# Eight weight chunks of the adaLN modulation move from VectorE to GpSimd and ScalarE inside the softmax heads

## The reference, cut to what matters

```
mod = silu(c) @ w_ada + b_ada            # 2048 x 12288, split into sh_a, sc_a, g_a, sh_m, sc_m, g_m
h = rms_norm(x) * (1 + sc_a) + sh_a ;  p = h @ w_in
A: latent attention, 8 heads (softmax)   B: stick-breaking, 8 heads   C: forgetting attention, 8 heads (softmax)
x = x + g_a * (concat(head norms of A, B, C) @ w_out)
h = rms_norm(x) * (1 + sc_m) + sh_m ;  x = x + g_m * (relu(h @ w1)^2 @ w2) ;  final rms_norm
```

## Time and profile before

| what | value |
|---|---|
| median of 3 runs | 1148.61 us (1147.33 to 1149.9) |
| the profiled execution's own time | 1150.71 us |
| its span in the trace | 1148.9 us |
| TensorE busy | 1101.0 us, 96% |
| VectorE busy | 724.6 us, 63% |
| ScalarE busy | 530.3 us, 46% |
| GpSimd busy | 309.3 us, 27% |

### The profile page before, as it was taken

One profiled execution on the slowest core, in us unless ns is written; L12 is line 12 of the kernel. 1 busy time (PEld: TensorE's weight loads), 2 busy tenths in 40 slices (PEclk: granted clock), 3 DMA queues, 4 the chain that ended last, 5 costly groups with the idle time before them and its releaser, 6 DMA issues.

```text
span 1148.9 us, 21562 instructions
## 1 busy us (share of the span) xinstructions
PE 1101.0 (96%) x9084; PEld 1072.9 (93%) x9084; DVE 724.6 (63%) x866; ACT 530.3 (46%) x657; POOL 309.3 (27%) x158
## 2 busy tenths in 40 slices
PE   7989999888999989999999999999999999999995
PEld 6889998886889989999999999999999999999995
DVE  5688676869886559787786444545555555445443
ACT  4644443564555445444544334343444444344341
POOL 3879996775138950000000000000000000000000
PEclk9999999999999998999999999999999999999998
DMA  9999998699777983888886565565556656555631
GB/s 382 416 415 415 415 400 331 220 347 376 249 256 288 410 310 131 301 287 296 291 301 204 190 201 188 198 191 196 192 192 200 191 187 202 196 190 194 199 117 74
DMA packets 76703, 296.87 MB, mean 258 GB/s; under 512 B 8512, under 2 KB 8640, under 8 KB 72512
## 3 DMA queue, kind: packets, MB, share of 16 engines
q1 hardware_dynamic: 76608, 295.50, 71.2%
HBM read 293.37 MB, written 2.10 MB: 257 GB/s over the span
## 4 chain that ended last, share of the span: by engine, by line
PE 80%; DMA 7%; DVE 6%; issue 4%; ACT 2%; SPq 0%; POOL 0%; DVEq 0%; ACTq 0%; POOLq 0%
PE ps L1310 50%; PE ps L1316 25%; DMA ada<-in_ada 4%; DMA ada_more<-in_whole 3%; PE ps L1328 2%; DVE ada L892 2%; PE ps L1492 1%; DMA ada<-in_whole 1%; PE ps L1333 1%; DVE qk L958 1%; ACT w_hi L465 1%; DVE ada_more L892 0%; DVE tmp L929 0%; ACT o_tok L698 0%; PE ps L1359 0%
## 5 line engine op out<-in xcount | busy, mean ns | idle before, releaser
L465 ACT ACTIVATE w_hi<-raw 128x1024 fp32r<-128x1024 f32 x362 | 380.6, 1059 | 466.2 <-PE ps L1316 420.5
L870 DVE TENSOR_TENSOR w_lo<-raw,w_hi 128x1024 fp32r<-128x1024 f32 x256 | 312.7, 1229 | 274.8 <-ACT w_hi L465 274.1
L1310 PE MATMUL ps<-hT,w_hi 128*128 128x256 f32 x3072 | 384.8, 278 | 12.7 <-issue 8.4
L1310 PEld LDWEIGHTS ps<-hT,w_hi 128*128 128x128 f32 x3072 | 367.2, 189 | 16.0 <-issue 9.5
L764 POOL TENSOR_TENSOR w_lo<-raw,w_hi 128x1024 fp32r<-128x1024 f32 x106 | 256.3, 2440 | 54.3 <-ACT w_hi L465 53.7
L1310 PE MATMUL ps<-act,w_hi 128*128 128x256 f32 x2048 | 253.2, 276 | 0.0
L1310 PEld LDWEIGHTS ps<-act,w_hi 128*128 128x128 f32 x2048 | 241.8, 188 | 0.1
L1316 PE MATMUL ps<-hT,w_lo 128*128 128x256 f32 x1536 | 207.4, 278 | 0.0
L758 POOL TENSOR_TENSOR ssq<-ssq,sq 128x1024 f32<-128x1024 f32 x6 | 14.4, 2404 | 658.2 <-ACT sq L472 658.2
L1316 PEld LDWEIGHTS ps<-hT,w_lo 128*128 128x128 f32 x1536 | 190.6, 189 | 0.0
L1316 PE MATMUL ps<-act,w_lo 128*128 128x256 f32 x1024 | 136.9, 276 | 0.0
(11 more groups left out here) (217 smaller groups left out, 797.4 us busy)
## 6 DMA issues: line engine op xcount, KB each, us to landing
raw<-in_weights SPq DMA_DIRECT2D x362, 512.0 KB, 4.5
ada<-in_ada SPq DMA_DIRECT2D x128, 512.0 KB, 5.4
ada<-in_whole SPq DMA_DIRECT2D x16, 1024.0 KB, 11.9
ada_more<-in_whole SPq DMA_DIRECT2D x16, 1024.0 KB, 12.7
xT<-in_xt SPq DMA_DIRECT2D x4, 512.0 KB, 7.1
y<-tmp SPq DMA_DIRECT2D x2, 512.0 KB, 2.8
consts<-in_consts SPq DMA_DIRECT2D x1, 580.0 KB, 9.8
y<-sq SPq DMA_DIRECT2D x1, 512.0 KB, 3.0
```

Of the source, the lines that this page charges most:

```text
L465: sc.activation(w_hi[:, u % RING, :, :], raw[:, u % LOADS, :, :], ACT.Copy).then_inc(hi_done, 1)
L870: ve.tensor_tensor(w_lo[:, slot, :, :], raw[:, u % LOADS, :, :], w_hi[:, slot, :, :].bitcast(F32), ALU.subtract).then_inc(lo_vec, 1)
L1310: pe.matmul(acc[:, n, :], w, rhs[:, kt0 + k, half, :], start=first and k == 0 and n % 2 == 0 and half == 0, stop=False, skip_group_check=True)
```

## The change

Eight of the twenty chunks among the softmax heads, the odd ones from 83 to 97, are taken out of DVE's queue. POOL multiplies chunk by `c` in place (`chunk_product`), with the SBUF copy `c_rep`; ACT then copies the buffer onto itself with an accumulator output (`sum_product`) into a column of `pool_sum`. Afterwards one DVE instruction adds the eight sums and their `plus_one` terms into `part_sum`. The load that reuses the buffer of such a chunk (`load_ada` of 87, 89, ..., 101) waits for ACT's sum instead of DVE's chunk. All other waits on `ada_done` are counted anew by `ada_count`.

POOL does products 0 and 1 after `fox_operand(7)`, products 2 to 5 between the two scalings by the head norm, and products 6 and 7 after the second. ACT does sum 0 at the end of step H+7, right behind `copy_pt(5)`, and the others in steps H+8, 9, 11, 13, 14, 16 and 17.

```diff
+POOL_AT, POOL_N = 33, 8
+SUM_AT = (7, 8, 9, 11, 13, 14, 16, 17)
+def pool_index(a):
+    m = a - A_X - POOL_AT
+    return m // 2 if 0 <= m < 2 * POOL_N and m % 2 == 0 else None
+def ada_count(a):
+    return sum(1 for n in range(a) if pool_index(n) is None)
...
             def load_ada(a):
-                if a >= WHOLE:
-                    sp.wait_ge(ada_done, ada_before(a) + 1)
+                n = pool_index(ada_before(a))
+                if n is not None:
+                    sp.wait_ge(pool_summed, n + 1)
+                elif a >= WHOLE:
+                    sp.wait_ge(ada_done, ada_count(ada_before(a) + 1))
...
+            def sum_product(n):
+                room = ada_room(A_X + POOL_AT + 2 * n)
+                sc.wait_ge(pool_made, n + 1)
+                sc.activation(room, room, ACT.Copy, accum_out=pool_sum[:, n:n + 1]).then_inc(pool_summed, 1)
...
                     copy_pt(t - H - TURN_LAG)
+                for n in range(POOL_N):
+                    if t == H + SUM_AT[n]:
+                        sum_product(n)
...
+            def chunk_product(n):
+                a = A_X + POOL_AT + 2 * n
+                gp.wait_ge(ada_landed(a), 16 * ada_round(a))
+                if n >= 2:
+                    gp.wait_ge(pool_made, n - 1)
+                gp.tensor_tensor(ada_room(a), ada_room(a), c_rep[:, D // 2:D], ALU.mult).then_inc(pool_made, 1)
+            gp.wait_ge(c_kept, 1)
+            chunk_product(0)
+            chunk_product(1)
             for n, at in enumerate((AT_SB, AT_FX)):
+                if n == 1:
+                    for i in range(2, POOL_N - 2):
+                        chunk_product(i)
                 gp.wait_ge(head_scaled, n + 1)
...
+            for n in range(POOL_N - 2, POOL_N):
+                chunk_product(n)
             for j in range(U_OUT - LAG):
                 lo(B_OUT + LAG + j)
...
             for t in range(STEPS):
-                todo = list(ada_at(t))
+                todo = [a for a in ada_at(t) if pool_index(a) is None]
...
+            ve.wait_ge(pool_summed, POOL_N)
+            ve.tensor_tensor(part_sum[:, POOL_AT:POOL_AT + 2 * POOL_N:2], pool_sum[:, :],
+                             plus_one[:, KT + 1:2 * KT:2], ALU.add).then_inc(pool_merged, 1)
+            ve.wait_ge(pool_merged, 1)
             out_lo(2)
...
-                    pe.wait_ge(ada_done, A_OUT)
+                    pe.wait_ge(ada_done, ada_count(A_OUT))
```

More of the change, by code:

```diff
@@ L189, in hybrid_block @@
         part_sum = sb("part_sum", [P, 6 * KT])
+        pool_sum = sb("pool_sum", [P, POOL_N])
         rstd = sb("rstd", [P, 2, S])
@@ L259, in hybrid_block @@
         ada_done = sem("ada_done")
+        pool_made, pool_summed, pool_merged = sem("pool_made"), sem("pool_summed"), sem("pool_merged")
         silu_step = sem("silu_step")
@@ L717, in _ @@
                 if j == 0:
-                    sc.wait_ge(ada_done, A_GM)
+                    sc.wait_ge(ada_done, ada_count(A_GM))
                 operand_hi(R_FFN + j, hT[:, 2 * j:2 * j + 2, :, :], mod[:, SH_M, 2 * j:2 * j + 2])
@@ L890, in ada_tile @@
                 if a >= 2:
-                    ve.wait_ge(ada_done, a - 1)
+                    ve.wait_ge(ada_done, ada_count(a) - 1)
                 ve.tensor_tensor_reduce(out=room, in0=room, scale=1.0,
@@ L915, in make_gain @@
             def make_gain(g, c, k0, n, last):
-                ve.wait_ge(ada_done, last + 1)
+                ve.wait_ge(ada_done, ada_count(last + 1))
                 ve.tensor_tensor(gain[:, k0:k0 + n], mod[:, g, k0:k0 + n], cols[:, c + k0:c + k0 + n],
@@ L1258, in _ @@
                 if half == 0:
-                    ve.wait_ge(ada_done, A_END)
+                    ve.wait_ge(ada_done, ada_count(A_END))
                 def down(it, last=False):
```

## The result

The changed kernel takes 1202.2 us (median of 4 runs, 1201.3 to 1206.2), the kernel before 1149.3 in the same comparison: a ratio of 1.047, with an interval of 1.0443 to 1.0497. The forecast was 1167 us, with a range up to 1176. The sign was right, and the loss is almost three times as large. The span of the profiled execution is 1200.4 us, 51.5 more than before. In the comparisons of the experiments 15 of 44 executions of the kernel before, one of four in experiment 2, two of four in experiment 4 and one of nine at distance 448 took some 23 to 30 us longer at an unchanged granted clock (the kernel before 1171 to 1178 us); the ratios leave them out, and no trace of one was kept.

The account below looks back on a forecast made before the run. PE, busy 96% of the span, was taken as the bound, with no slack to recover delays among the heads. Loads 13.4, clock 2.7 and POOL against DVE 2.4 made 18.5 us on 1148.6: 1167 us, range 1157 to 1176.

Parts of the forecast that it names:

- From `out_lo(2)` on the work is as before: Everything behind out_lo(2), before at 333.73 us: no further cost; from 390 us on all as before, 15 to 22 us later.
- The heads: Softmax heads and last head norm: late loads, lower clock and POOL holding DVE cost 18.5 us together, +12 to +25.
- The loads: Among the heads: loads queued behind ACT's late sums delay DVE's chunks, making out_lo(2) start 13.4 us late.
- The clock: Behind PE's 6 to 7 us pause, about 341 to 348 us: lower clock costs 2.7 us once, ends 0 and 6.
- POOL against DVE: Newton steps, chunks 99, 100: POOL's instruction holds two-SBUF-operand DVE instructions (the lock); one hold, 2.4 us, ends 0 and 7.1.
- the cheaper case: Among the heads: same waits partly covered, no clock or lock cost; +2 to 9.4 us, 1151 to 1160; 13 in 100.
- the dearer case: Among the heads: lower clock several times, POOL holds DVE at each meeting; +26.5 us and above, 1174 and more; 9 in 100.
- Faster: Heads 13 and 14 and out_unit(0): DVE's relief and chunk 97 gone bring 1146.5 to 1147.5 us; 5 in 100.
- no change: Loads hidden among the heads, only sum 7 on the path behind copy 15: +0.3 us, 1149; 3 in 100.
- DVE's relief: Softmax heads: eight chunks leaving DVE remove 9.6 us of its work, winning at most about 1.1 us.

Follow-up runs that it names:

- experiment 2: The changed kernel with pool_sum as a view of the existing tensor small, so no tensor moves: ratio 1.0182 to the kernel before.
- experiment 4: The kernel before plus the eight products and sums on two spare buffers, results unused, all chunks on DVE, loads released as before: ratio 1.003.
- distance 448: The kernel before with row and small allocated ahead of raw, making the weights-to-moving-operand distance 448 modulo 512: 1148.8 us, ratio 0.9998.
- Experiments 1: The kernel before with one unused 32-byte tensor allocated behind part_sum, where the change puts pool_sum: 1184.3 us, ratio 1.0313.
- Experiment 3: The kernel of experiment 2 without its products and sums; POOL and ACT only signal, the loads still wait: 1162.4 us, ratio 1.0123.
- experiment 5: The kernel of experiment 2 with three own buffers for the eight chunks, loads reordered, product 6, last sum and addition moved: 1147.5 us, ratio 1.0.

## Why the prediction was wrong

**The step that failed** is the sentence "From `out_lo(2)` on the work is as before", with its companion that from 390 us on all would be as before and only later. The work is as before; its speed isn't. The new tensor of 32 bytes had no term in the sum, since it costs no instruction. It moved `hT`, `oT` and `act` against the weights from distance 192 to 224, and the pitch from 113.3 to 118.3 ns. The MLP has 256 units of 24 matmuls: 6144 times 5.0 ns is 30.7 us, beside the 28.8 that the span has more from the first latent `out_turn` on. Experiments 1 and 2 show it from both sides, with 35 us for the tensor alone and 20 for the change without it. No rival held this either, so the range failed with the sum.

**The heads** were forecast at 18.5 us and cost 21.2, within the forecast's own +12 to +25. The mechanism held:

- *The loads.* Forecast: DVE idles for landings ahead of chunks 88, 92, 94, 96 and 99. It does ahead of 88, 94, 96 and 99, with 3 to 7 us each, not ahead of 92, and with 1.7 us ahead of 90, which wasn't forecast. PE's pauses stand before heads 10 and 14 and before the late `out_turn`, as forecast. From head 8 to `out_lo(2)` it is 50.4 us now and was 32.3: 18.1 more, where the loads' 13.4 and the lock's 2.4 made 15.8. Experiment 3 shows the cause of most of it: signals without work cost 14 us. The work alone made 6.2 us among the heads (experiment 4). With the late signals undone and the last product and sum moved as well, nothing was left (experiment 5); which of these moves took the 6 us away wasn't tested singly.
- *The clock.* The unit behind the long pause takes 5.14 us (355.07 to 360.21) instead of 2.8 (335.13 to 337.95): 2.3, forecast 2.7. It happened among the heads too, which I had kept for the upper end: from head 10 to head 11 it is 4.63 us, which before was 2.98 (306.74 to 309.72). The granted clock is 0.78 on average from 349 to 372 us, a stretch with the pause in it. From `out_lo(2)` to the two `out_turn` it is 18.3 us against 15.1 before, 3.1 more. With the 18.1 ahead of it that is the 21.2.
- *POOL against DVE.* Chunk 99 took 3.32 us instead of 1.27, chunk 100 1.63, and a Newton step of the first norm 2.25 instead of 0.17; POOL was at a `w_lo` or a product each time. Forecast was one hold of 2.4 on the path. Chunk 99 and 100 make 2.4 directly ahead of `out_lo(2)`. The Newton step stands ahead of a DVE that waited for chunk 88 until 309.00 anyway. The Trainium skill's rule (SBUF — State Buffer, section "SBUF: two separate sides") agrees with the rows: only instructions with two SBUF inputs were held, chunks that read `c` from PSUM stayed at 1.28. A held instruction counts as busy, so DVE's busy time fell by 5.3 us (724.6 to 719.3) and not by the 9 to 10 forecast.

**Two slips in the bounds.** The middle of the cheaper case, 1151 to 1160, is 1155.5 and not the 1157 that the range begins with; and 26.5 us on 1148.6 is 1175, where the dearer case begins with 1174. Neither matters beside a miss of 35.

**The rivals.** "Faster" and "no change" had 8 in 100 together and were rightly low: even with the waits undone (experiment 5) DVE's relief of 9.6 us yields 1.1 us among the heads, the most that the prediction gave it, and nothing in the times. "Dearer", at 26.5 us and above, had the sign of the miss but not its mechanism: the heads stayed at 21.2.

## What to carry to other kernels

A new tensor is a change of its own, however small: compare the pitch of the untouched matmuls in one window of a late stage, matmuls over time, before reading anything else. Do it in more than one execution and in more than one stage, since the same layout can show two values. If it moved while the clock didn't, look at what the allocation moved, and put the new tensor into space that shifts nothing.

When work moves from one engine to another, the buffer's release moves with it. Ask where in the new engine's queue the release stands, and what is queued behind the transfer that waits for it. Here a chunk that nobody needed soon held up the load of one that DVE wanted next. A buffer of its own and an issue order by need took that away.

## What the runs showed of the hardware

- The pitch of fp32r matmuls with 256 columns, each with a new weight load, depends on where tensors lie relative to each other in SBUF, by the likeliest reading the stationary and the moving operand: in the MLP 113.3 ns at 192 and 448 bytes modulo 512, and 117.7 to 119.9 at the eight other distances tried. Moving both together changes nothing. That the two reads get in each other's way is the obvious reading; no run shows the inside of it. The Trainium skill (TensorE: Matmul & The Clock Gate, section "Step-by-step: what each phase is for") says that the two operands have read ports of their own and that loading the next weights takes no SBUF bandwidth from the running matmul. These runs show a cost that one wouldn't expect from that: the same instructions take 4 to 6% longer in the MLP by position, and the measurement decides, though it doesn't say where the cost arises.
- Whether the pattern repeats every 256 bytes stays open, and so does whether a distance that isn't among the ten is better.
- At one distance the pitch isn't always one number. At 192 the output projection of the kernel before runs at 117.8 ns and its MLP at 113.3; in the kernel of experiment 5 both run at 113.3. At 320 it is 113.3 in the projection and 117.7 in the MLP, at 384 118.7 and 119.9. So what sets the MLP at 64 and 320 apart from that at 192 and 448 may not be the distance as such, but which of two values it falls into; the seven executions at 64 and 320 took 1174.6 to 1181.1 us. What decides it was not found.
